# Prompt attention of a hybrid decoder step on one Trainium2 core: the work of the next pair of heads moved into the pair before it

## The reference

```python
q = (c_q @ w_q_up).reshape(B, L, N_HEADS, D_NOPE + D_ROPE)        # 16 heads, 64 + 32
kv = (c_kv @ w_kv_up).reshape(B, L, N_HEADS, D_NOPE + D_V)
for blk in range(L // Q_BLOCK):                                   # four blocks of 128 queries
    s = (q_nope[:, q0:q1] . k_nope[:, :q1] + q_pe[:, q0:q1] . k_pe[:, :q1]) * scale
    p = softmax(where(mask, s, -inf))
    outs.append(p @ v[:, :q1])
```

## Time and profile before

| | us |
|---|---|
| median of 3 runs (lowest to highest) | 1593.4 (1583.5 to 1593.8) |
| span of the profiled execution | 1590.6 |
| span of the eight pairs in it, first query product to first transpose of the decode side | 79.4 to 315.3 |

### The profile page before, as it was taken

How to read it: one execution, slowest core, us unless ns; L and a number is a source line. 1 busy time by engine, 2 the same in 40 slices (tenths; PEclk the granted TensorE clock), 3 DMA queues, 4 the chain that set the end, 5 groups by cost and what they waited for, 6 DMA issues and landing times.

```text
span 1590.6 us, 32114 instructions
## 1 busy us (share of the span) xinstructions
PE 1497.3 (94%) x11463; PEld 1418.5 (89%) x11463; DVE 772.5 (49%) x1234; ACT 603.5 (38%) x1085; POOL 356.2 (22%) x422
## 2 busy tenths in 40 slices
PE   5978998889999999999999998789999999999997
PEld 5966676688887999999999998789999999999997
DVE  3876656555553543442334454964444423344332
ACT  6444545475553333311233333342333311233233
POOL 0286776344310002200022132000012200122000
PEclk9999999999999999999999999889999999999998
DMA  7123323333433123223232565512222232222321
GB/s 178 24 59 87 100 79 101 111 97 91 116 91 116 55 84 88 79 85 87 71 87 79 179 153 159 191 35 80 79 80 79 79 93 79 80 79 85 87 67 60
DMA packets 245283, 147.62 MB, mean 93 GB/s; under 512 B 42072, under 2 KB 239615, under 8 KB 244191
## 3 DMA queue, kind: packets, MB, share of 16 engines
q1 hardware_dynamic: 237826, 138.35, 30.1%
q0 software_dynamic: 6704, 7.20, 1.8%
q10 hardware_dynamic: 684, 1.18, 0.2%
HBM read 128.42 MB, written 18.26 MB: 92 GB/s over the span
## 4 chain that ended last, share of the span: by engine, by line
PE 85%; DVE 8%; ACT 3%; issue 3%; DMA 1%; SPq 0%; ACTq 0%; DVEq 0%
PE bank L856 62%; PE bank L776 7%; PE bank L1114 3%; PE bank L1079 3%; PE bank L919 2%; PE bank L979 2%; PE bank L936 1%; PE bank L967 1%; DVE arena L2050 1%; DVE tmpa L2339 1%; ACT arena L1375 1%; DVE arena L2366 1%; DVE sq L2339 1%; DVE tmpa L2048 1%; DVE tmpa L2047 1%
## 5 line engine op out<-in xcount | busy, mean ns | idle before, releaser
L856 PE MATMUL bank<-arena_parts,wR 128*128 128x288 f32 x4224 | 566.0, 296 | 4.2 <-ACT arena_parts L1452 3.7
L856 PEld LDWEIGHTS bank<-arena_parts,wR 128*128 128x128 f32 x4224 | 562.9, 188 | 5.2 <-issue 4.9
L856 PE MATMUL bank<-side_parts,wR 128*128 128x288 f32 x3360 | 447.3, 295 | 1.1 <-DVE tmpa L2411 1.1
L856 PEld LDWEIGHTS bank<-side_parts,wR 128*128 128x128 f32 x3360 | 445.5, 188 | 1.5 <-issue 1.3
L1859 DVE TENSOR_TENSOR wR<-wraw,wR 128x1024 fp32r<-128x1024 f32 x159 | 232.8, 1464 | 241.5 <-ACT wR L1438 240.1
L741 POOL TENSOR_TENSOR arena_parts<-sq,arena_parts 128x576 f32 x64 | 91.6, 1431 | 729.8 <-ACT arena_parts L1669 729.8
L1438 ACT ACTIVATE wR<-wraw 128x1024 fp32r<-128x1024 f32 x159 | 167.0, 1050 | 202.0 <-PE bank L856 187.5
L1375 ACT ACTIVATE arena<-bank 128x256 f32<-128x256 f32 (+9 forms) x223 | 95.3, 443 | 135.0 <-PE bank L776 87.9
L1666 ACT ACTIVATE tmpa<-bank 128x576 f32<-128x576 f32 x64 | 41.7, 651 | 195.5 <-PE bank L856 195.5
L2262 DVE TENSOR_TENSOR sq<-tmpa 128x576 f32<-128x576 f32 x64 | 48.5, 759 | 127.2 <-ACT tmpa L1666 127.2
L2190 DVE TENSOR_TENSOR kpR<-bank,rstd 128x576 f32<-128x576 f32 x32 | 24.2, 758 | 127.9 <-PE bank L856 127.9
(11 more groups left out here) (300 smaller groups left out, 1604.6 us busy)
## 6 DMA issues: line engine op xcount, KB each, us to landing
wraw<-in_mlp_w SPq DMA_DIRECT2D x128, 512.0 KB, 4.0
side<-in_cache_ckv SPq DMA_DIRECT2D x128, 128.0 KB, 2.1
wraw<-in_ssm_w_glu SPq DMA_DIRECT2D x16, 512.0 KB, 4.0
s_state_to_out<-side SPq DMA_DIRECT2D x16, 256.0 KB, 2.5
s_in_to_state<-yblk SPq DMA_DIRECT2D x8, 512.0 KB, 2.6
s_in_to_out<-side SPq DMA_DIRECT2D x64, 64.0 KB
wraw<-in_mla_w_o SPq DMA_DIRECT2D x8, 512.0 KB, 5.2
side<-s_in_to_state SPq DMA_DIRECT2D x2, 2048.0 KB, 13.2
```

The source lines that it names most:

```text
L856: return pe.matmul(bank[:, a, 0:HALF], wR[:, s, wp, k, :], tokens(k, xp)[:, a * HALF:(a + 1) * HALF], start=(first and j == 0), stop=(last ...
```

## The change

The same products and copies are made, in another order, and with a second set of buffers for the queries (`qT[1]` is the tile `sq`) and the keys (`kT[1]` lies in `acc` and in `side`). The first pair's queries, keys, values and turned key weights stand ahead of the loop. Then, in each pair p:

- the values' product and the turn of the key weights of p are the first work on PE, into `bank7` and `bank6`, and DVE's copy of the values stands before its scaling of unit 0;
- the lag products of pair p-1 come behind the turn of unit 0, the latent queries of p behind them;
- the keys of p+1 are made behind the turn of unit 2 and its values;
- the query product of head 0 of p+1 comes behind the scores of unit 6, that of head 1 behind the turn of unit 5, both into `bank67`; DVE's four instructions for each stand before its `unit_scale` of unit 5 and of unit 7;
- the scores of units 0 and 1 of p+1 come behind the turns of units 6 and 7 of p;
- `chunk_turn` is second to last, before the values of the last block; it goes into `bank6` and `bank7`, and the next pair's values wait for ACT's copy of them.

The third score bank moves from `bank6` to `bank45[:, 1]`. The query weights get their own semaphore (`wq_in`) and are loaded a pair earlier, behind `chunk_out`; `chunk_out` is that of p-1; the key pages are issued by SP instead of POOL; POOL makes the rest of the query weights of p+1 at the start of its chunk p. The rotary key rows are copied to both key buffers (four copies at L2013 instead of two). The loops of PE, DVE and ACT run over two pairs at a time, three times. The core of the diff:

```diff
-        score_banks = [bank01[:, 0, :], bank01[:, 1, :], bank6[:, :]]
+        score_banks = [bank01[:, 0, :], bank01[:, 1, :], bank45[:, 1, :]]
@@ SP
+            with sp.Fori(1, PAIRS - 2) as p:
                 sp.wait_ge(uk_done, p + 1 + CREDIT)
                 apart(sp)
                 pair_weights(p + 1)
                 first_pages(p)
-                chunk_out(p)
+                chunk_out(p - 1)
+                sp.wait_ge(wq_lo, p * 6 + 12)
+                apart(sp)
+                query_weights(p + 2)
@@ POOL
-                if not isinstance(p, int):
-                    rest_of_weights(p)
+                if not last:
+                    rest_of_weights(p + 1)
@@ PE
+            def pair_of_heads(p, par, first=False, last=False):
+                if not first:
+                    pe.wait_ge(yt_sb, p + CREDIT)
+                    values_product()
+                    turn_up_keys(bank6)
+                unit_scores(p, par, 2)
+                unit_turn(p, 0)
+                if not first:
+                    pe.wait_ge(v_sb, p + 1)
+                    chunk_lags(p - 1)
+                latent_queries(p, par)
+                unit_scores(p, par, 3)
+                unit_turn(p, 1)
+                unit_scores(p, par, 4)
+                unit_turn(p, 2)
+                pair_values(p, 0)
+                if not last:
+                    pe.wait_ge(ql_sb, p * 4 + 4 + CREDIT)
+                    keys_product(p + 1)
+                unit_scores(p, par, 5)
+                unit_turn(p, 3)
+                unit_scores(p, par, 6)
+                if not last:
+                    pe.wait_ge(k_sb, p * 2 + 4)
...
+                    query_product(p + 1, 0, bank67)
+                unit_turn(p, 4)
+                pair_values(p, 2)
+                unit_scores(p, par, 7)
+                unit_turn(p, 5)
+                if not last:
+                    pe.wait_ge(qn_sb, p * 2 + 3)
+                    pe.wait_ge(qr_sb, p * 2 + 3)
+                    query_product(p + 1, 1, bank67)
+                unit_turn(p, 6)
+                if not last:
+                    unit_scores(p + 1, 1 - par, 0)
+                pair_values(p, 4)
+                unit_turn(p, 7)
+                if not last:
+                    unit_scores(p + 1, 1 - par, 1)
+                chunk_turn(p, last)
                 pair_values(p, 6)
...
+            chunk_lags(PAIRS - 1)
@@ ACT
+            def pair_of_heads(p, par, first=False, last=False):
+                if not first:
+                    up_keys_out(p, bank6)
+                unit_turned(p, 0)
+                unit_exp(p, 2)
+                if not last:
+                    cut_queries_of(p + 1)
+                chunk_inputs(p)
...
+                unit_turned(p, 2)
+                unit_exp(p, 4)
+                if not last:
+                    keys_out(p + 1, 1 - par)
...
+                unit_turned(p, 7)
+                if not last:
+                    unit_exp(p + 1, 1)
+                chunk_turned(p)
                 heads_out(p)
@@ DVE
+            def pair_of_heads(p, par, first=False, last=False):
+                if not first:
+                    values_out(p)
+                unit_scale(p, 0)
+                unit_max(p, 2)
+                if not first:
+                    lags_out(p - 1)
+                latent_queries(p)
...
+                unit_scale(p, 4)
+                unit_max(p, 6)
+                if not last:
+                    queries_out(p + 1, 1 - par, 0, bank67)
+                unit_scale(p, 5)
+                unit_max(p, 7)
+                unit_scale(p, 6)
+                if not last:
+                    queries_out(p + 1, 1 - par, 1, bank67)
+                unit_scale(p, 7)
+                if not last:
+                    unit_max(p + 1, 0)
+                    unit_max(p + 1, 1)
+                    rotary_rows(p + 1, 1 - par)
```

More of the change, by code:

```diff
@@ L969, in keys_product, with query_product @@
                 ins.then_inc(k_done, 1)
-            def pair_of_heads(p, last):
-                pe.wait_ge(hw_in, p * 96 + 96)
+            def query_product(p, h, banks):
                 pe.wait_ge(wq_lo, p * 6 + 6)
[L974 to L993, removed]
@@ new lines, in query_product, with values_product @@
+                for a in range(2):
+                    cols = slice(a * HALF, (a + 1) * HALF)
+                    for j, (w, x) in enumerate(((wqH, HI), (wqH, LO), (wqL, HI))):
+                        for k in range(4):
+                            ins = pe.matmul(banks[:, a, 0:HALF], w[:, k, h, :], cqH[:, k, cols] if x == HI else cq_lo[k][a],
+                                            start=(j == k == 0), stop=(j == 2 and k == 3))
+                ins.then_inc(q_done, 1)
+            def values_product():
@@ new lines, in _ @@
+            for h in range(2):
+                query_product(0, h, pair[h])
+            pe.wait_ge(h_ready, H_CKV + 2)
+            pe.wait_ge(var_ready, 2)
+            keys_product(0)
+            values_product()
+            turn_up_keys(bank45[:, 0, :])
+            pe.wait_ge(kpe_raw, 1)
+            unit_scores(0, 0, 0)
+            unit_scores(0, 0, 1)
+            pair_of_heads(0, 0, first=True)
+            with pe.Fori(0, PAIRS // 2 - 1) as i:
+                pair_of_heads(i * 2 + 1, 1)
+                pair_of_heads(i * 2 + 2, 0)
@@ L1555, in pages_turned @@
+            keys_out(0, 0)
+            up_keys_out(0, bank45[:, 0, :])
+            unit_exp(0, 0)
+            unit_exp(0, 1)
+            pair_of_heads(0, 0, first=True)
+            with act.Fori(0, PAIRS // 2 - 1) as i:
+                pair_of_heads(i * 2 + 1, 1)
+                pair_of_heads(i * 2 + 2, 0)
+            pair_of_heads(PAIRS - 1, 1, last=True)
             def pages_turned(b, par, g):
@@ L2065, in _ @@
[L2065 to L2073 removed]
+                                    qT[par][64:96, h, SEQ:N].unsqueeze(2)).then_inc(ql_sb, 1)
@@ L2078, in _ @@
                 dve.tensor_copy(kdc[:, P + GS:2 * P], bank7[:, GS:P]).then_inc(kd_sb, 1)
-                step.leave(PAIRS)
+            def pair_of_heads(p, par, first=False, last=False):
[6 more added lines that the diff above has]
+                latent_queries(p)
+                unit_scale(p, 1)
+                unit_max(p, 3)
+                unit_scale(p, 2)
+                unit_max(p, 4)
+                unit_scale(p, 3)
+                unit_max(p, 5)
+                unit_scale(p, 4)
[8 more added lines that the diff above has]
+                unit_scale(p, 7)
+                if not last:
+                    unit_max(p + 1, 0)
+                    unit_max(p + 1, 1)
+                    rotary_rows(p + 1, 1 - par)
+            for h in range(2):
+                queries_out(0, 0, h, pair[h])
+            unit_max(0, 0)
+            rotary_rows(0, 0)
+            unit_max(0, 1)
+            values_out(0)
+            pair_of_heads(0, 0, first=True)
+            with dve.Fori(0, PAIRS // 2 - 1) as i:
+                step.enter(i, 2 * (4 + 8))
+                pair_of_heads(i * 2 + 1, 1)
+                pair_of_heads(i * 2 + 2, 0)
+                step.leave(PAIRS // 2 - 1)
+            pair_of_heads(PAIRS - 1, 1, last=True)
+            lags_out(PAIRS - 1)
             dve.wait_ge(s_done, 8 * PAIRS)
```

216 lines of the change are left out of this document (113 added, 103 removed).

## The result

| | us |
|---|---|
| changed kernel, median of 4 runs (lowest to highest) | 1630.4 (1627.8 to 1631.7) |
| before, median of 4 runs | 1593.5 (1583.5 to 1593.8) |
| ratio, 95% interval | 1.0249 (1.0219 to 1.0279) |
| span of the profiled execution, after and before | 1629.3 and 1590.6 |

The time lies inside the predicted range, 10 us above the predicted value. In what follows the spans are compared: +38.7 us, where the sum in the prediction made +28.4.

The account below looks back on a forecast made before the run. PE was taken to bound the kernel, busy 24.60 of 27.45 us a pair. Terms +18.0, +1.2, -3.9 and +0.9 gave 1606.8 us at full clock; +12.2 for the clock gave 1619, written 1620, range 1600 to 1636.

Parts of the forecast that it names:

- The pair at full clock: One steady-state pair on PE: 24.6 us busy plus 6.0 idle, 30.6 us; over seven pairs +18.0 us.
- Stall A: PE idle before the turn of unit 5, whose scaling stands behind DVE's read-out of head 0's queries: 2.6 us a pair.
- Stall B: PE idle before the turn of unit 7, whose scaling stands behind DVE's read-out of head 1's queries: 2.7 us a pair.
- Turns 0 and 1: PE's waits for DVE's scaling before the turns of units 0 and 1: 0.7 us a pair for both.
- The values' product: PE's wait, before the next values' product, for ACT's copies of the state-space turns: 0.1 us a pair.
- The other queues: Key weight loads, ACT's and POOL's query weight work, SP's key pages: delays hidden, costed at nothing.
- The clock: TensorE falling to half rate behind the long stalls: about 9 of 14 bring a fall, 1.36 us each, +12.2 us.
- Rival 2: The stalls come but TensorE's clock stays: 1600 to 1612 us, about 1608; chance 0.22.
- Rival 3: All 14 stalls bring a clock fall, with L2050 long in each Stall A: 1632 us, up to 1640; chance 0.13.
- The prologue: Ahead of pair 0's turn of unit 1: two more DVE copies, +1.6 us, less 0.4 taken back, +1.2.
- The last pair: Pair 7 makes no queries: 2.7 us of half clock and 1.2 us of two waits go, -3.9 us.
- The tail: Pair 7's lag products come last, so decode page loads start 2.9 us later against 2 us of slack: +0.9 us.

Follow-up runs that it names:

- the run with four fillers: Changed kernel plus unread PE products before four turns a pair: 8 (unit 5), 11 (unit 7), 2 each (units 0, 1); 1604.0 us, ratio 1.0093.
- the run with 16 and 22 products: Changed kernel plus products nobody reads on PE, 16 before the turn of unit 5 and 22 before that of unit 7; 1629.4 us, ratio 1.0274.
- the second experiment: Changed kernel, but DVE scales unit 5 before reading out head 0's queries, unit 7's scaling left as it was; 1627.0 us, ratio 1.0253.

## Why the prediction was right, and where it was off

| stretch | predicted | measured |
|---|---|---|
| up to the turn of unit 1 in pair 0 | +1.2 | -3.4 |
| seven pairs, at full clock | +18.0 | +18.1 |
| seven pairs, for the clock | +12.2 | +24.8 |
| turn of unit 1 in pair 7 to the decode side | -3.9 | -0.95 |
| from there on | +0.9 | +0.1 |
| sum | +28.4 | +38.7 |

The measured pairs at full clock are those of the run with four fillers: six of 30.52 us and the last of 31.2 make 214.3, and 214.3 - 196.2 = 18.1; 239.15 - 214.3 = 24.8 is the clock's. Seven pairs at full clock keep PE busy for 7 x 24.6 = 172.2 us; the changed kernel's 196.1 are 23.9 more, so nearly all of the clock's 24.8 is busy time made longer. (The kernel before had a little of that itself, 174.0.)

**The pair at full clock: right.** 30.6 us were forecast, 30.5 measured. Stall A: 2.6 forecast, 2.0 to 2.9 measured, and 2.03 in four of the seven pairs. Stall B: 2.7, and 2.7 to 3.1. Turns 0 and 1: 0.7 for both, and 0.43 + 0.51. The values' product: 0.1, and at most 0.24. The mechanism and each term hold; that the sum is so close owes something to stall A being shorter and the small waits longer than forecast. The sign of the result follows from these alone. The other queues cost nothing, as said. In pair 7 neither stall A nor B came; the 1.30 us before its turn of unit 7 stood there in the kernel before too.

**The clock: the term that was mis-sized.** The step failed at "I expect about 9 of them to bring a fall, at the 1.36 us that one cost". In the changed kernel TensorE ran at half clock for 58 us of the seven pairs, in stretches whose lengths add up to 17 times 3.41 us (thirteen whole falls, three of them double, and the rest of one that began ahead of the first turn of unit 1); that is 24.8 / 17 = 1.5 us each, near the 1.36. So it was the count that failed, in three ways. Of the 14 stalls 11 brought a fall, where I had expected 9. I counted falls where time at half clock should have been counted: two of the 11 are twice as long, as the one of 6.83 us in the last pair had shown, so these stalls stand for 13 of the 17. And the turns of units 0 and 1 were priced for their idle time but not counted as a place of falls, though the falls of the kernel before stood behind just such waits, as the prediction itself had said; two falls within the seven pairs, one of them double, began at the turn of unit 1, 3 of the 17. The last of the 17 is that rest. Rival 2, in which the clock stays, is refuted for this kernel by the 0.88 of its row; what it would have given is what the run with four fillers gave, 1604.0 us, within the 1600 to 1612 stated. Rival 3 came near in the count of falls: 11 of 14 stalls.

**The prologue: wrong sign.** The step was DVE's two more copies, "median 0.81", +1.6. The nearest row was one taken beside POOL's products, and the change took POOL away from that place: the four copies took 0.4 each, and the whole stretch of DVE ran unhindered. I had the range of that row, 0.41 to 1.22, and had named POOL as the cause for L2050, but did not ask where POOL would be. PE's idle time there shrank from 6.34 us to 0.91 and 2.48. Moving POOL's tables back ahead of it turned the gain into a loss.

**The last pair.** Of the 1.2 us for waits that go, 0.95 were there (PE's idle time went from 2.8 to 2.1 us), but not the 2.7 for the clock: the row of the last stretch shows a granted clock of 0.79 against 0.80 before. I had given the fall back since its waits go; another one came in its place. Which wait brings it was not tried.

**The tail.** PE in order of time in the changed kernel, where it wants the first pages of the decode requests:

```profile
375.44 0.66 PE L798 MATMUL bank<-ident,arena_parts 128*96 128x128 f32 x2 [2.43 <-DMA side<-in_cache_ckv]
```

The pages are late, for 2.43 us where it had been 0.17, more than the forecast +0.9. Yet the span from the first transpose of the decode side to the end is longer by only 0.1 us. So the wait is real and was given back later; where, I did not try, and it stays open.

The errors, measured minus predicted: -4.6 in the prologue, +0.1 in the pairs, +12.6 for the clock, +2.95 in the last pair, -0.8 in the tail, in sum +10.3. Part of the closeness is luck: without the error in the prologue, the sum would have been 15 us short.

## What to carry to other kernels

When work of the next stage is moved into this one, look at the order of each engine that reads the result, not only of the one that makes it: an instruction that is ready must not stand behind one that has yet to wait, however idle that engine looks on average. Price every idle time of TensorE twice, for itself and for the slow products that may stand behind it, and keep the half-microsecond waits among the candidates. A handful of products that nobody reads in each wait tells the clock's part from the wait's, and was worth 24.6 us here without any other edit.

## What the runs showed of the hardware

- With the long stalls filled, TensorE's clock still went from 2.4 to 1.2 GHz for 3.4 to 6.8 us, five times, each time at a wait of half a microsecond. Two products of 0.23 us in each of the two short waits of a pair ended it. The length of a wait alone doesn't tell: 0.44 and 0.53 us brought no fall in the run with 16 and 22 products, 0.81 and 0.48 us one in seven pairs of the kernel before.
- The falls can come back in every pair. In the last pairs of the second experiment the clock fell at the same places of each pair, 10.2 us a pair, and what stall A was shorter by, some 0.7 to 1.6 us in each pair (2.03 to 2.88, then 1.26 to 1.30), was worth nothing.
- DVE's instructions on SBUF were 2.4 to 3.6 times as long beside POOL's products (two copies of 32x512: 0.76 and 2.46 us; a single one: 0.41 and 1.49; a product of 64x576: 0.74 and 1.81), and one that reads PSUM was not (0.75 in both). The Trainium skill (GPSIMD Engine Reference, "1. Specifications") has GpSimd share VectorE's SBUF interfaces, with contention for VectorE's instructions that use a two-port mode or have two SBUF inputs. The trace agrees for the product, which has two inputs, with 1.81 us against 0.74; of the copy no run shows whether it uses such a mode.
